# A layer's expert output and final norm, laid out by token instead of by feature, on one Trainium2 core

## The reference

```python
x = x + mixing_block(h, ...)                     # ends in mix @ w_out
h = rmsnorm(x, norm_ffn_w)
# peer_ffn: 8 heads choose 16 of 128*128 experts per token
top_s, pos = lax.top_k(cand_s, PEER_TOPK)
gate = jax.nn.softmax(top_s, axis=-1)
act = gelu(einsum('td,tkd->tk', xt, u[it]))      # u: 16384 x 2048
out = einsum('tk,tkd->td', gate * act, v[it])    # v: 16384 x 2048
x = x + out
return rmsnorm(x, final_norm_w)
```

## Time and profile before

| what | value |
|---|---|
| time, median of 3 runs | 5205.21 us (5199.18 to 5206.64) |
| time of the profiled execution | 5234.92 us |
| its span | 5232.2 us |
| mean granted clock of TensorE in it | 0.971 of 2.4 GHz |
| TensorE busy | 4945.5 us, 95% of the span |
| VectorE, ScalarE, GpSimd busy | 3275.9, 1503.2, 1661.0 us |
| U stage, V stage, norm stage final | from 2656 to 4094, from 4096 to 5192, from 5193 to the end |

### The profile page before, as it was taken

How to read it: one execution, slowest core, us unless ns; L and a number is a source line. 1 busy time by engine, 2 the same in 40 slices (tenths; PEclk the granted TensorE clock), 3 DMA queues, 4 the chain that set the end, 5 groups by cost and what they waited for, 6 DMA issues and landing times. The chain is left out here.

```text
span 5232.2 us, 69516 instructions
## 1 busy us (share of the span) xinstructions
PE 4945.5 (95%) x25836; PEld 4450.6 (85%) x25836; DVE 3275.9 (63%) x4660; ACT 1503.2 (29%) x1236; POOL 1661.0 (32%) x560
## 2 busy tenths in 40 slices
PE   6999979999999999998969989999999799999997
PEld 5877767888887787887769889999999799999997
DVE  3566666888887101001058879997443688888886
ACT  2232223333333322112223234443222222222222
POOL 2333320000000343443334455557888311111111
PEclk6999989999999999999989999999999899999999
DMA  1222212222221333334223357777878888888884
GB/s 70 90 87 84 88 48 89 77 85 76 86 83 65 131 108 141 113 120 157 88 110 115 106 216 261 261 260 290 303 297 308 312 300 300 299 302 299 302 301 152
DMA packets 230891, 913.30 MB, mean 175 GB/s; under 512 B 18352, under 2 KB 100912, under 8 KB 152624
## 3 DMA queue, kind: packets, MB, share of 16 engines
q1 hardware_dynamic: 193968, 644.12, 35.1%
q0 software_dynamic: 36864, 268.45, 13.9%
HBM read 837.00 MB, written 75.50 MB: 174 GB/s over the span
## 5 line engine op out<-in xcount | busy, mean ns | idle before, releaser
L158 POOL TENSOR_TENSOR ring_low<-ring_raw,ring_high 128x2048 fp32r<-128x2048 f32 x273 | 1294.9, 4744 | 2295.7 <-ACT ring_high L153 2295.0
L176 PE MATMUL rt_acc<-h_high,ring_high 128*128 128x384 f32 (+1 forms) x2304 | 793.6, 344 | 22.9 <-POOL ring_low L158 20.7
L177 PE MATMUL rt_acc<-h_low,ring_high 128*128 128x384 f32 (+1 forms) x2304 | 785.9, 341 | 0.0
L178 PE MATMUL rt_acc<-h_high,ring_low 128*128 128x384 f32 (+1 forms) x2304 | 785.9, 341 | 0.0
L153 ACT ACTIVATE ring_high<-ring_raw 128x2048 fp32r<-128x2048 f32 x337 | 645.4, 1915 | 388.8 <-PE out_acc L178 125.1
L1740 DVE CUSTOM_DVE_ANT_0 sb_rt_rows<-sb_rt_rows,sb_rt_h_tok 128x2048 f32<-128x2048 f32 x128 | 334.2, 2611 | 280.3 <-DMA sb_rt_rows<-u_rows,row_of 277.0
L176 PEld LDWEIGHTS rt_acc<-h_high,ring_high 128*128 128x128 f32 x2304 | 434.1, 188 | 38.6 <-POOL ring_low L158 17.0
L177 PEld LDWEIGHTS rt_acc<-h_low,ring_high 128*128 128x128 f32 x2304 | 434.1, 188 | 9.9
L178 PEld LDWEIGHTS rt_acc<-h_high,ring_low 128*128 128x128 f32 x2304 | 433.7, 188 | 10.1
L1364 POOL DMA_INDIRECT sb_op_rows<-v_tiles,row_of x128 | 122.8, 959 | 945.4 <-DVE sb_op_total L1905 922.3
L176 PE MATMUL hg_acc<-h_high,ring_high 128*128 128x512 f32 x1024 | 408.4, 399 | 9.2 <-DVEq L968 9.2
(11 more groups left out here) (298 smaller groups left out, 9909.6 us busy)
## 6 DMA issues: line engine op xcount, KB each, us to landing
ring_raw<-u_tiles SPq DMA_DIRECT2D x128, 1024.0 KB
ring_raw<-v_tiles SPq DMA_DIRECT2D x128, 1024.0 KB
ring_raw<-w_hg SPq DMA_DIRECT2D x64, 1024.0 KB
ring_raw<-w_ssd SPq DMA_DIRECT2D x48, 1024.0 KB
ring_raw<-w_mix_s SPq DMA_DIRECT2D x32, 1024.0 KB
ring_raw<-w_mix_h SPq DMA_DIRECT2D x32, 1024.0 KB
gelu<-sb_rt_gelu SPq DMA_DIRECT2D x128, 192.0 KB
gates<-sb_rt_table SPq DMA_DIRECT2D x12, 2048.0 KB, 8.5
```

What stands on the lines that cost most here:

```text
L158: nc.gpsimd.tensor_tensor(ring.low[:, slot], ring.raw[:, slot], ring.high[:, slot].bitcast(F32), ALU.subtract).then_inc(ring.low_ready, 1)
L176: nc.tensor.matmul(out, high[:, m], x_high[:, k, tokens], start=(k == 0), stop=False, skip_group_check=True)
L177: nc.tensor.matmul(out, high[:, m], x_low[:, k, tokens], start=False, stop=False, skip_group_check=True)
L178: last = nc.tensor.matmul(out, low[:, m], x_high[:, k, tokens], start=False, stop=(k == KT - 1), skip_group_check=True)
```

## The change

Four things change together.

1. The V stage works token by token. The stationary operand is now a 128 by 128 block of the weights (128 experts, 128 tokens), the moving one 512 features of V. An output is 128 tokens by 512 features; a half of a group has 6 outputs (3 token blocks by 2), each of 12 matmuls, over 8 banks in turn. The gathered rows of the first 128 tokens are added straight into x (`x_tok`), without `sb_op_total` and without transposes behind. For this, x must stand token on partition: `out_stage` transposes every tile on TensorE (4 transposes of 128x128 each), ScalarE copies it, and SyncE stores it in pieces of 512 bytes; the store of x_mid in the ffn norm falls away. x_tok is loaded in two halves of 2 MB.
2. The final norm is part of the V stage: VectorE sums the squares of each token's row and multiplies, ScalarE takes the root of 128x1, SyncE stores 8 pieces of 512 KB. The norm stage "final" is gone.
3. The weights of group 0 are loaded, multiplied and split in the U stage, before its last pair of tiles, and a group's inputs are asked for behind the first two tiles of the group before.
4. The U gathers end four tiles earlier (76 of them over 56 tiles, before over 60).

```diff
@@ out_stage
+            def store(n, slot):
+                sp.wait_ge(turn_read, n + 3)
+                sp.dma_start(x_tok[:, :, ds(P * n, P)], tok[:, slot]).then_inc(tok_stored[slot], 16)
...
+            def keep(n, slot, before):
+                act.wait_ge(turned, n + 1)
+                act.wait_ge(tok_stored[slot], 16 * before)
+                nc.scalar.activation(tok[:, slot], ps_turn[slot][:], ACT.Copy).then_inc(turn_read, 1)
...
+            def turn(n, slot):
+                pe.wait_ge(added, n + 3)
+                pe.wait_ge(turn_read, n + 1)
+                for c in range(NC):
+                    last = nc.tensor.transpose(ps_turn[slot][:, c], x_mid[:, n, c * P:(c + 1) * P], const["ident"])
+                last.then_inc(turned, 1)
...
@@ route_stage
-            return GATE_TILES + SLOTS + (HK - GATE_TILES - SLOTS) * (i - GATE_TILES) // LATE
+            late = min(i - GATE_TILES, LATE - SLOTS)
+            return GATE_TILES + SLOTS + (HK - GATE_TILES - SLOTS) * late // (LATE - SLOTS)
...
+            weights.load(sp, scratch, 0, v_landed)
             turn(PAIRS - 2, 1)
             load_ahead(sp, ring, FIRST + 2 * PAIRS, following)
             turn(PAIRS - 1, 0)
...
+            act.wait_ge(v_weighted, 1)
+            nc.scalar.activation(weights.high0, weights.w, ACT.Copy).then_inc(v_split, 1)
+            pair(PAIRS - 1)
...
+            dve.wait_ge(v_landed, 32)
+            weights.weigh(vec).then_inc(v_weighted, 1)
+            dve.wait_ge(v_split, 1)
+            vec.tensor_tensor(weights.low0, weights.w, weights.high0.bitcast(F32), ALU.subtract)
...
@@ output_stage
-        OUTS = 8
+        BANKS = 8
+        BLOCKS = REST // CH
+        HALF = D // 2
+        OUTS = 2 * BLOCKS
...
-                            nc.tensor.matmul(o, v_high[s][:, m], w_high[:, buf, j], start=(j == 0), stop=False)
...
+                            if i == 0 and j % 2 == 0:
+                                pe.wait_ge(ring.low_ready, ring.base + 4 * g + (s + 1))
+                            m = slice(j % 2 * HALF + i % 2 * T, j % 2 * HALF + (i % 2 + 1) * T)
+                            high, low = w_high[buf][:, j, toks], w_low[buf][:, j, toks]
+                            nc.tensor.matmul(o, high, v_high[s][:, m], start=(j == 0), stop=False)
...
+            def group(g, buf, static):
+                for half in range(2):
+                    if static and g == 0:
+                        dve.wait_ge(x_landed[half], 16)
+                    for i in range(OUTS):
+                        s = 2 * half + i // 3
+                        if i in (0, 3):
+                            low(4 * g + (s + 2), (s + 2) % 4)
...
+                            elif g > 0:
+                                row(5 * g + (s - 3))
...
-        norm_stage(nc, "final", x_mid, vecs["final_norm_w"], work, const["ones"], const["eps"], store=out)
```

336 lines of the change are left out of this document (217 added, 119 removed).

## The result

The changed kernel takes 5194.27 us (median of 20 runs, 5158.04 to 5201.32), the kernel before 5232.81 in the same comparison (20 runs, 5199.18 to 5242.09): ratio 0.9931, 95% interval 0.9913 to 0.9949. The spans of the profiled executions went from 5232.2 to 5191.5 us, **-40.7 us**; forecast were -55.4. The predicted time, 5149.8 us, and its range, 5136 to 5168, were missed.

A forecast was written before the change was run, and what follows sets the result against it. It took TensorE, busy for 95% of the span, as the bound: -20.8 - 16.4 - 0.5 - 30.9 + 7.7 + 4 + 1.5 = -55.4 us, from the 5205.2 median to 5149.8. Range with rivals 5136 to 5168, its own 5143 to 5156.

The forecast's parts named there:

- Part 6: U stage: denser gathers +1 us, ScalarE's split of the first V weights +0.5, wait for `v_weighted` nothing; together +1.5.
- Part 1: V stage: fewer, 512-column matmuls at the mix stage's step of 226.7 ns, cost beyond columns one per matmul: -20.8 us.
- rival A: V stage: cost beyond columns grows by 3.7 ns with V as moving operand, step gains only 3.8: 5167 us; chance 0.06.
- Part 2: V stage: VectorE keeps up with TensorE inside a group; cost 0, bound +1 us for each of six groups.
- Part 3: U to V border: stages meet and TensorE starts earlier, -16.4 us; stand before group 0's second half slightly shorter, -0.5.
- rival C: U to V border: transfers rule, x lands at 4119 and a second tile wait comes: +7 to +14, 5157 to 5164; chance 0.13.
- Part 4: Tail: from the last V matmul to the span's end 14.6 us instead of 45.5: -30.9 us.
- Part 5: Out stage: 64 transposes on TensorE's path +7.7 us, last transposes, copy and store at the stage's end +4.

The follow-up runs named there:

- e1: Changed kernel with ScalarE's split of group 0's V weights moved from ahead of the last U pair to between its two tiles: 5192.11 us, ratio 0.9933.
- e7: Changed kernel with U gathers again running to the U stage's end and the first V-weight split behind the last U pair: 5202.44 us, ratio 0.9911.
- e8: Changed kernel with the even groups' rounded weights, from group 2 on, at lower bytes 179488 to 191776: 5176.73 us, ratio 0.9896.
- e10: Changed kernel with the even groups' high and low weight tensors exchanged at their high place: 5162.04 us, one run.
- e11: Kernel of e8 with the even groups' high and low weight tensors exchanged at the low place: 5190.44 us, one run.
- e2: Changed kernel with GpSimd's first V gather held until the first half of x has landed: 5186.74 us, ratio 0.9928.
- e4: Changed kernel without the out stage's transposes, copies and stores of x_tok, x loaded from another input: 5182.81 us, ratio 0.9919.

## Why the prediction was wrong, and where it was right

**The failed step is the carrying over: "from the median of the runs 5205.2 - 55.4 = 5149.8".** The profiled execution was 29.7 us above those three runs, and I treated the difference as a shift without a cause. It is a second level, on which most runs lie (14 of 20 before, 17 of 20 after). The same sum against the profile's own time gave 5179.5, and the range would have gone from 5166 to 5198; the median measured, 5194.3, lies in it. Against the lower level the three runs after, 5158 to 5161, lie inside the range that was given. As a difference -55.4 was still too much, by 14.7 us in the profile: 11.4 in the V stage and 7.0 in the U stage were missed, and 3.7 came back in the three other rows of the first table.

*Part 6, the U stage: "I keep 1.5 for both". Failed: it measured 8.5.* Two things are in it. ScalarE's wait for `v_weighted` was to be nothing, since "the last dot ends 12 us after its gather's tile"; it was 2.15 us, and with the split itself it cost 4 us, as e1 showed. Behind it stands a dot that takes three times its length. GpSimd and VectorE in time order:

```profile
4073.23 5.28 POOL L188 TENSOR_TENSOR ring_low<-ring_raw,ring_high 128x2048 fp32r<-128x2048 f32 x1 [1.84 <-ACT ring_high L183]
```
```profile
4074.56 6.10 DVE L1811 CUSTOM_DVE_ANT_0 sb_rt_rows<-sb_rt_rows,sb_rt_h_tok 128x2048 f32<-128x2048 f32 x1 [0.23 <-DMA sb_rt_rows<-u_rows,row_of]
4080.59 0.08 DVE L1811 DVE_READ_ACCUMULATOR2_ANT sb_rt_dot<- 128x1 f32 x1
4081.00 1.76 DVE L137 TENSOR_TENSOR weights_w<-weights_gelu,weights_gate 128x1536 f32<-128x1536 f32 x1
```

The split ends at 4078.51 and the dot 2.15 us later; the dot before this one, at 4071.74, with no split beside it, took 2.29 in all: it had stood until GpSimd was done. Without the 3.8 us of that, ScalarE's wait of 2.15 would not have come up. The Trainium skill (SBUF — State Buffer, "Who interferes with whom") has this as a rule: a VectorE instruction with two inputs in SBUF and a GpSimd instruction that reads SBUF exclude each other, and the one that comes second blocks for the whole of the first. The rows agree. Another 4.1 us came up between the 65th and the 125th tile, mostly in stands for `ring_low` of U tiles; between executions they vary by as much, and whether the denser gathers cause them stays open (e7).

*Part 1, the step: right in kind, 1.1 ns too small.* Not the shape of the moving operand (rival A) but the place of one pair of weights, 0.32 us in every second group, some 5 us in all (e8, e10, e11): nearly half of the 11.4 us that the V stage missed. With both pairs low the period is 32.64 us, 226.7 ns a matmul, exactly the mix stage's step; so the idea that the cost beyond columns is one per matmul held for the new operands. The Trainium skill's smaller gap of N / 2.4 + 2.5 ns (TensorE: Matmul & The Clock Gate, "Back-to-back issue gap"), which that section gives for an isolated matmul, did not hold in this stream: it gives 215.8 ns where 226.7 were measured.

*Part 2, VectorE: right.* The trace has no wait of TensorE after 4160.

*Part 3, the border: the mechanism right, the second stand too small.* The meeting took 4.6 us, where 5.9 were reckoned (13.9 less 8.0), and stands of 2.0 and of 8.9 + 2.7 were there where "about 3 and 8" were forecast. What was missed is the order of the transfers: x was to come 24 us after 4088 with everything at 400 GB/s, and came 29 us after the V stage's start, rival C in part. e2 shows the four gathers as the cause. The clock's fall I had counted for the first stand only; from 4140 to 4150 it shows again: 20 matmuls in 7.33 busy us at a granted clock of 0.57, which take 4.5 at the full step. The longer stand (11.6 for 8.4 us) and this fall, some 3 us each, are the rest of what the V stage missed.

*Part 4, the tail: right,* 13.8 us against 14.6. *Part 5, the out stage: right,* 10.1 against 11.7, and e4 gives 10.1 for the stage alone. (64 transposes at 0.123 us would be 7.9 and not the 7.7 of the sum; measured were 0.47 us a tile, 7.5.)

## What to carry to other kernels

When the profiled execution and the timed runs lie further apart than repeated runs do, find the difference in the trace before carrying a sum over, for it may be a second level of the same program. At a border between stages, transfers that nobody needs yet (here gathers that free buffers allowed) are paid for by those that are needed; a wait on the landing of what is needed costs one line. GpSimd's splits and VectorE's dots and `hot` tensors were not two parallel costs but one after the other, and where such an operation stands ahead of a chain, count it with the other engine's length added. Compare runs only with those of the kernel before in the same comparison: here its level moved by 3 us between comparisons, where effects of 4 us were sought.
